# Input projections of a two-layer encoder trunk: the 512 columns of a matmul walked in alternating ways instead of in order

## The chip, the cores and the metric

The kernel runs on one core of one Trainium2 chip. The metric is the device time of one execution, in microseconds (us), smaller is better.

## What is computed

Two residual layers over a stream `x` of 256 tokens by 2048 columns, all in fp32. Each layer norms the stream, multiplies it by one combined input projection, runs a token mixer (layer 0: differential attention with 16 heads; layer 1: a spatial gating MLP) and, beside it, a 4-head attention into 256 memory tokens, and maps both back by one output projection. A SwiGLU feed-forward part follows.

```python
for i in range(DEPTH):                      # DEPTH = 2
    h = rms_norm(x, norm_mix_g[i])          # (256, 2048)
    mem_n = rms_norm(mem, norm_mem_g[i])
    if m == 0:
        p = h @ a_w_in[j]                   # 2048 x (6144 + 512)
        tok = diff_attention(p[..., :A_PROJ], ...)
        xq, w_out = p[..., A_PROJ:], a_w_out[j]
    elif m == 1:
        p = h @ b_w_in[j]                   # 2048 x (4096 + 512)
        tok = spatial_gating_mlp(p[..., :B_PROJ], ...)
        xq, w_out = p[..., B_PROJ:], b_w_out[j]
    cross = memory_attention(xq, mem_n, ...)
    x = x + jnp.concatenate([tok, cross], axis=-1) @ w_out
    x = x + swiglu(rms_norm(x, norm_ffn_g[i]), ffn_w_gate[i], ffn_w_up[i], ffn_w_down[i])
```

The two lines `p = h @ ...` are the input projections.

## The kernel before

**Number format.** A product of two fp32 matrices is made of three matmuls in a rounded fp32 type (`F32R`, fp32r in the profile): each factor is split into a high part and a low part, and high by high, high by low and low by high are summed in PSUM.

**Blocks.** The output columns of a projection are cut into blocks of 512, the width of one PSUM bank of fp32. Layer 0 has 13 blocks (`A_BLOCKS`: one for the memory queries, then four groups of keys, queries, values), layer 1 has 9 (`B_BLOCKS`). A block runs over 8 chunks (`IN_CHUNKS`) of the contraction; a chunk is two tiles of 128 rows of weights, 512 KB. For each chunk, `product` issues 2 contraction tiles x 2 token tiles x 3 matmuls = 12 matmuls, so a block has 96 and the 22 blocks have 2112. In each of them the stationary operand is a 128x128 tile of the transposed stream (`hT_hi`, `hT_lo`), the moving operand is 128 rows by 512 columns of split weights (`w_hi` or `w_lo`), read in order of address, and the result is added into the 512 columns of a bank, in order of address. `run_block` also issues, between chunks, the transposes and the attention steps that belong to earlier blocks.

**Supply.** The order of all instructions is written out by hand, engine by engine. SyncE loads a chunk of raw weights into a ring of four places, ScalarE rounds it to `w_hi` (L1061), VectorE subtracts to get `w_lo` (L1504), and TensorE waits for `chunk_split` before the first matmul of a chunk. Its last matmul counts up `chunk_used`, which lets ScalarE and VectorE write that place again. The banks of a block are read by ScalarE and VectorE while TensorE works on the next block in two others; these reads don't look at the order in which the columns were written.

The same function `product` also serves the key and value projections of the memory, the output projection of layer 0 and most units of the feed-forward part. In all of these the columns are taken in order.

Of the kernel before, what the change touches and what calls it, by code (L numbers as in the profile page):

```python
# [51 lines left out]
IN_CHUNKS = KT // CHUNK_KT  # L52
# [39 lines left out]
END_SUM_T = (END_SUM[1] + 1, END_SUM[1] + 3)  # L92
AHEAD = 3
HOOK = 4
CROSS_HOOK = 7


# [136 lines left out]
def trunk(nc, x, mem, rel_bias, norm_mix_g, norm_mem_g, norm_ffn_g, mem_w_kv, mem_q_norm_g,  # L234
# [4 lines left out]
    with ctx:  # L239
# [13 lines left out]
        w_hi = sb("w_hi", [P, RING, CHUNK_KT, BLOCK], F32R)  # L253
        w_lo = sb("w_lo", [P, RING, CHUNK_KT, BLOCK], F32R)
# [131 lines left out]
        bank = [ctx.enter_context(nc.psum_tensor(f"bank{i}", [P, BLOCK], F32)) for i in range(8)]  # L386
# [76 lines left out]
        def ring_place(tally):  # L463

            n = tally.n["chunk"]
            ring_turn = n // RING
            if tally.turn is not None:
                ring_turn = tally.turn * (tally.per_turn["chunk"] // RING) + ring_turn
            return ring_turn, n % RING
# [45 lines left out]
        def layer_steps(layer, b, cross_step, diff_step):  # L515


            if b in ((2, 3), (3, 4))[layer]:
                return (lambda c: cross_step(IN_CHUNKS * (b - 2 - layer) + c)) if cross_step else None, CROSS_HOOK
            if layer == 0 and b >= 4:  # L520
                group, third = divmod(b - 4, 3)
                return (lambda c: diff_step(group, IN_CHUNKS * third + c)), DIFF_HOOKS[third]
            return None, HOOK

        def outputs_due(layer, b):

            if (layer, b) in ((0, 4), (1, 5)):
                return [("cross_out", layer)]
            if layer == 0 and b in (7, 10):
                return [("outputs", (b - 7) // 3)]  # L530
            return []
# [73 lines left out]
        def _(pe):  # L605
# [3 lines left out]

            asked = dict(cross_scores=0, diff_scores=0, transposed=0)  # L610

            def product(side_T, outs, c, order, first, last_one, ready=(), token_first=False):

                hi, lo = side_T
                _, slot = ring_place(tally)
                pe.wait_ge(chunk_split, tally.at("chunk", 1))
                if c in ready:
                    pe.wait_ge(T_free, tally.at("t"))  # L620
                steps = [(a, t) for a in range(CHUNK_KT) for t in range(TOK)]
                if token_first:
                    steps.sort(key=lambda at: at[1])
                for a, t in steps:
                    k = order[c] * CHUNK_KT + a
                    rows = slice(t * P, (t + 1) * P)
                    o = bank[outs[t]][:, :]
                    nc.tensor.matmul(o, hi[:, k, rows], w_hi[:, slot, a, :], start=(first and a == 0), stop=False)  # L628
                    nc.tensor.matmul(o, hi[:, k, rows], w_lo[:, slot, a, :], start=False, stop=False)  # L629
                    last = nc.tensor.matmul(o, lo[:, k, rows], w_hi[:, slot, a, :], start=False,  # L630
                                            stop=(last_one and a == CHUNK_KT - 1))
                    if token_first and (a, t) == (CHUNK_KT - 1, 0):
                        last.then_inc(first_token_done, 1)
                last.then_inc(chunk_used, 1)
                tally.add("chunk")
# [100 lines left out]
                                                v_b[:, t, h * P:(h + 1) * P], start=True, stop=True)  # L736
                last.then_inc(mixed, 1)

            def run_block(previous, side_T, chunks, ready=(), steps=None, hook=HOOK, order=None, end=False):

                base = 2 * parity[0]
                parity[0] ^= 1
                for c in range(chunks):
                    if steps is not None:
                        steps(c)
                    for kind, j in previous:
                        if kind == "gated":
                            if c == hook:
                                mix(j)
                            elif c == hook + 2:  # L750
                                transpose4(y_tile)
                        elif c == hook:
                            after(kind, j)
                    product(side_T, (base, base + 1), c, order or range(chunks), c == 0, c == chunks - 1, ready,
                            token_first=(end and c == chunks - 1))


            def three(o, hi, lo, weight_hi, weight_lo, first, last_one):
# [170 lines left out]
            stream_T = (hT_hi, hT_lo)  # L929
# [55 lines left out]
            previous = [("mem_values", 1)]  # L985

            for layer, blocks in enumerate((A_BLOCKS, B_BLOCKS)):
                for b, (kind, j, _) in enumerate(blocks):
                    steps, hook = layer_steps(layer, b, lambda at: cross_step(layer, at), diff_step)
                    previous += outputs_due(layer, b)  # L990

                    run_block(previous, stream_T, IN_CHUNKS, ((0,) if layer == 0 else (6,)) if b == 0 else (), steps, hook)
                    previous = [(kind, j)]

                if layer == 0:

                    previous += [("outputs", QT - 2)]
                    bases = (2 * parity[0], 2 * (parity[0] ^ 1))
                    for i, (b, c) in enumerate(TAIL_CHUNKS):
                        diff_step(QT - 1, i, tail_steps)  # L1000
                        if i == HOOK + 1:
                            for p in previous:
                                after(*p)
                        product(mixer_T, (bases[b], bases[b] + 1), c, OUT_ORDER, c == 0, False, (0, OUT_SPARE) if b == 0 else ())
                    diff_step(QT - 1, 2 * OUT_EARLY, tail_steps)


                    wait(pe, s_free, HEADS)
                    t_banks[0] = O_BANKS
                    bases += (T_BANKS,)  # L1010
                    for i, (b, c) in enumerate(END_CHUNKS):
                        if i == END_TRANSPOSE:
                            after("outputs", QT - 1)
                        if i in END_SUM_T:
                            after("stream", END_SUM_T.index(i))
                        product(mixer_T, (bases[b], bases[b] + 1), c, OUT_ORDER, c == 0, c == OUT_CHUNKS - 1,
                                (OUT_EARLY,) if b == 0 else ())
                    t_banks[0] = T_BANKS
                    run_block([("stream", 2)], mixer_T, OUT_CHUNKS, order=OUT_ORDER)
                    banks = (2 * parity[0], 2 * (parity[0] ^ 1))  # L1020
                    events = {HOOK: [("stream", 3)]}
                else:
                    banks = (2 * parity[0], 2 * (parity[0] ^ 1))
                    run_pair(PAIRS + 1, OUT[0], mixer_T, out_sets[0], banks, {HOOK: [("mix", QT - 1)], HOOK + 2: [("gated", QT - 1)]},
                             fresh=True, order=OUT_ORDER)
                    run_pair(PAIRS, OUT[1], mixer_T, out_sets[1], banks, {OUT_HOOKS[0]: [("stream", 0)], OUT_HOOKS[1]: [("stream", 1)]},
                             fresh=True, order=OUT_ORDER)
                    events = {OUT_HOOKS[0]: [("stream", 2)], OUT_HOOKS[1]: [("stream", 3)]}

                run_pair(0, plan_of(0), stream_T, buffers(0), banks, events, fresh=True)  # L1030
                hidden = {GATE_HOOK: [("hidden", 0)]}
                with pe.Fori(0, (LATE - 2) // TURN_PAIRS) as turn:
                    tally.enter(turn)
                    for pair in (1, 2):
                        run_pair(pair, plan_of(pair), stream_T, buffers(pair), banks, hidden)
                    tally.leave((LATE - 2) // TURN_PAIRS)
                for pair in range(LATE - 1, PAIRS):
                    run_pair(pair, plan_of(pair), stream_T, buffers(pair), banks, hidden)
                run_pair(PAIRS, DOWN[0], hidden_T, down_sums[0], banks, hidden, fresh=True)
                if layer == 0:  # L1040
                    events = {HOOK: [("stream", 0)], DOWN_NEXT: [("stream", 1)],
                              DOWN_DONE_T: [("collected", 0), ("stream", 2)]}
                else:
                    events = {DOWN_NEXT: [("final", 1)]}
                run_pair(PAIRS + 1, DOWN[1], hidden_T, down_sums[1], banks, events, fresh=True, end=(layer == 1))
                parity[0] ^= 1
                previous = [("stream", QT - 1)]
# [1130 lines left out]
```

## Time and profile before

| | |
|---|---|
| median of 2 runs | 2346.77 us (2346.41 to 2347.14) |
| span of the profiled execution | 2345.2 us, from its first to its last instruction |
| TensorE (PE) busy in it | 2338.7 us |
| VectorE (DVE) busy | 1828.8 us |
| ScalarE (ACT) busy | 1267.7 us |
| DMA | 449.52 MB, mean 192 GB/s |

The profile is of one execution of its own. It gives the span; no other time of that execution is given, so the span stands for it, 1.6 us under the median of the runs. A line such as "L628 PE MATMUL bank<-w_hi,hT_hi 128*128 128x512 f32 x1600" is a group of instructions: line of the kernel, engine, operation, what is written and read, the stationary tile, the moving tile, and how many there are. The duration of a matmul in such a line runs from its start to the end of its drain, and the next one starts before that. How long the engine needs per matmul is therefore read from the distance between two starts in the timeline.

### The profile page before, as it was taken

How to read it: one execution, taken by the hardware profiler on the slowest of the kernel's cores; microseconds unless marked ns; L12 is line 12 of the kernel's file. 1: busy time of each engine (PE TensorE's matmuls, PEld its weight loads, DVE VectorE, ACT ScalarE, POOL GpSimd, SP SyncE). 2: the span in 40 equal slices, each digit the busy share in tenths (PEclk: the TensorE clock that was granted, in tenths of full speed). 3: DMA queues.
4: the chain of work that ended last, by engine and by line, in shares of the span. 5: the costliest groups of instructions: out<-in, count | busy, mean ns of one | idle time of the engine just before them, and what ended most of it. 6: DMA issues, size and time to landing. Idle time of an engine off the chain costs nothing.

```text
span 2345.2 us, 29322 instructions
## 1 busy us (share of the span) xinstructions
PE 2338.7 (100%) x10530; PEld 1895.1 (81%) x10530; DVE 1828.8 (78%) x2257; ACT 1267.7 (54%) x1572; POOL 171.3 (7%) x120
## 2 busy tenths in 40 slices
PE   9999999999999999999999999999999999999999
PEld 7888888888888888888888888888888888888887
DVE  6555666656988888889998546689988888889987
ACT  7645555545655555555564454455655555555553
POOL 1000110000111121110000000000111111100000
PEclk9999999999999999999999999999999999999999
DMA  8665555456665666666656755556665666667664
GB/s 262 208 188 154 162 162 162 157 167 205 205 191 188 198 194 188 200 195 227 198 184 201 234 157 167 179 180 202 206 202 185 198 191 187 198 196 227 201 206 156
DMA packets 235043, 449.52 MB, mean 192 GB/s; under 512 B 14893, under 2 KB 19122, under 8 KB 234674
## 3 DMA queue, kind: packets, MB, share of 16 engines
q1 hardware_dynamic: 224274, 430.01, 58.4%
q10 hardware_dynamic: 10656, 18.00, 2.2%
q8 instruction: 71, 1.16, 0.2%
q14 instruction: 42, 0.34, 0.0%
HBM read 441.64 MB, written 6.32 MB: 191 GB/s over the span
## 4 chain that ended last, share of the span: by engine, by line
PE 98%; ACT 1%; DVE 1%; issue 0%; POOL 0%; ACTq 0%; POOLq 0%; DVEq 0%
PE bank L630 24%; PE bank L628 24%; PE bank L629 24%; PE bank L759 7%; PE bank L761 7%; PE bank L760 7%; PE bank L684 2%; PE bank L881 1%; PE bank L649 0%; PE bank L906 0%; PE bank L735 0%; PE bank L855 0%; PE bank L830 0%; ACT w_hi L1061 0%; PE bank L893 0%
## 5 line engine op out<-in xcount | busy, mean ns | idle before, releaser
L1504 DVE TENSOR_TENSOR w_lo<-raw,w_hi 128x1024 fp32r<-128x1024 f32 (+1 forms) x816 | 951.0, 1181 | 443.7 <-ACT w_hi L1061 441.6
L1061 ACT ACTIVATE w_hi<-raw 128x1024 fp32r<-128x1024 f32 (+1 forms) x815 | 812.9, 1007 | 754.2 <-PE bank L630 704.1
L628 PE MATMUL bank<-w_hi,hT_hi 128*128 128x512 f32 x1600 | 639.2, 400 | 0.0
L630 PE MATMUL bank<-w_hi,hT_lo 128*128 128x512 f32 x1600 | 635.0, 397 | 0.0
L629 PE MATMUL bank<-w_lo,hT_hi 128*128 128x512 f32 x1600 | 630.7, 394 | 0.0
L630 PEld LDWEIGHTS bank<-w_hi,hT_lo 128*128 128x128 f32 x1600 | 300.4, 188 | 71.8
L629 PEld LDWEIGHTS bank<-w_lo,hT_hi 128*128 128x128 f32 x1600 | 300.7, 188 | 71.4
L628 PEld LDWEIGHTS bank<-w_hi,hT_hi 128*128 128x128 f32 x1600 | 300.5, 188 | 69.5
L628 PE MATMUL bank<-w_hi,aT_hi 128*128 128x512 f32 x864 | 344.6, 399 | 0.0
L630 PE MATMUL bank<-w_hi,aT_lo 128*128 128x512 f32 x864 | 341.4, 395 | 0.0
L629 PE MATMUL bank<-w_lo,aT_hi 128*128 128x512 f32 x864 | 340.5, 394 | 0.0
L630 PEld LDWEIGHTS bank<-w_hi,aT_lo 128*128 128x128 f32 x864 | 162.2, 188 | 40.1
L629 PEld LDWEIGHTS bank<-w_lo,aT_hi 128*128 128x128 f32 x864 | 162.3, 188 | 38.2
L628 PEld LDWEIGHTS bank<-w_hi,aT_hi 128*128 128x128 f32 x864 | 162.2, 188 | 37.7
L1067 ACT ACTIVATE aT_hi<-sum_raw 128x2048 fp32r<-128x2048 f32 x52 | 99.5, 1914 | 76.7 <-DVE sum_raw L1524 75.2
L1531 DVE TENSOR_TENSOR aT_lo<-sum_raw,aT_hi 128x2048 fp32r<-128x2048 f32 x52 | 119.0, 2289 | 8.2 <-ACT aT_hi L1067 8.2
L2106 POOL TENSOR_TENSOR sum_raw<-raw 128x1024 f32<-128x1024 f32 x16 | 39.6, 2475 | 571.4 <-DMA raw<-in_ffn_w_up_dram 571.4
L2134 POOL TENSOR_TENSOR pow_out<-pow_in,halves 128x8 f32<-128x8 f32 (+1 forms) x16 | 40.8, 2552 | 397.0 <-DVE pow_in L1572 397.0
L759 PE MATMUL bank<-aT_hi,mix_hi 128*128 128x512 f32 x174 | 69.0, 397 | 0.0
L760 PE MATMUL bank<-aT_lo,mix_hi 128*128 128x512 f32 x174 | 68.8, 395 | 0.0
L761 PE MATMUL bank<-aT_hi,mix_lo 128*128 128x512 f32 x174 | 68.7, 395 | 0.0
L2134 POOL TENSOR_TENSOR rstd<-pow_in,halves 128x2 f32<-128x2 f32 x6 | 5.5, 914 | 757.5 <-DVE pow_in L1572 757.5
(237 smaller groups left out, 2595.0 us busy)
## 6 DMA issues: line engine op xcount, KB each, us to landing
raw<-in_ffn_w_gate_dram SPq DMA_DIRECT2D x176, 512.0 KB, 3.8
raw<-in_ffn_w_up_dram SPq DMA_DIRECT2D x176, 512.0 KB, 4.5
raw<-in_ffn_w_down_dram SPq DMA_DIRECT2D x176, 512.0 KB, 4.6
raw<-in_a_w_in_dram SPq DMA_DIRECT2D x104, 512.0 KB, 3.8
raw<-in_b_w_in_dram SPq DMA_DIRECT2D x72, 512.0 KB, 3.8
raw<-in_a_w_out_dram SPq DMA_DIRECT2D x40, 512.0 KB, 3.7
raw<-in_b_w_out_dram SPq DMA_DIRECT2D x40, 512.0 KB, 4.2
raw<-in_mem_w_kv_dram SPq DMA_DIRECT2D x32, 512.0 KB, 5.1
```

The lines of the kernel that those rows point to most:

```text
L628: nc.tensor.matmul(o, hi[:, k, rows], w_hi[:, slot, a, :], start=(first and a == 0), stop=False)
L629: nc.tensor.matmul(o, hi[:, k, rows], w_lo[:, slot, a, :], start=False, stop=False)
L630: last = nc.tensor.matmul(o, lo[:, k, rows], w_hi[:, slot, a, :], start=False, stop=(last_one and a == CHUNK_KT - 1))
L684: last = nc.tensor.transpose(ktile(t_banks[0], a)[:, t * P:(t + 1) * P], tile(t, a), ident[:, :])
L759: nc.tensor.matmul(o, hi, weight_hi, start=first, stop=False)
L760: nc.tensor.matmul(o, hi, weight_lo, start=False, stop=False)
L761: return nc.tensor.matmul(o, lo, weight_hi, start=False, stop=last_one)
L1061: nc.scalar.activation(w_hi[:, slot, 0:tiles], raw[:, slot, 0:tiles], ACT.Copy).then_inc(hi_ready, 1)
L1067: nc.scalar.activation(weights[0], weights[2][:, :, :], ACT.Copy).then_inc(sums_hi, 1)
L1504: nc.vector.tensor_tensor(w_lo[:, slot, 0:tiles], raw[:, slot, 0:tiles], w_hi[:, slot, 0:tiles].bitcast(F32), ALU.subtract).then_inc(chunk ...
L1531: nc.vector.tensor_tensor(lo, total[:, :, :], hi.bitcast(F32), ALU.subtract).then_inc(sums_split, 1)
L2134: nc.gpsimd.tensor_tensor(dest, pow_in[:, q % 2, 0:count], halves[:, 0:count], ALU.pow).then_inc(pow_given, 1)
```

## The change

A table `WALKS` gives each block of the input projections a walk: None, or a pair (ways, run). `walked` views the 512 columns as `ways` equal parts, and takes `run` neighbouring columns of the first part, then `run` of the second, and so on, then the next `run` of the first. The moving operand and the bank are both walked so, so each column still meets its own sum. Nothing else is changed: the stationary operand, the number of matmuls and the order of all instructions stay.

Of the 22 blocks three have None. In three more, (2, 256), (4, 128) and (8, 64), ways x run is 512, so each part is taken whole and the order is that of the addresses. The other 16 blocks jump: layer 0 from its third block on with (2, 128), (2, 64), (2, 32), (2, 16), (2, 8), (2, 4), (2, 2), (4, 16), (4, 2), (8, 2), (16, 2), and layer 1 in its third to seventh block with (4, 32), (4, 8), (8, 16), (16, 16), (32, 2).

```diff
+WALKS = ((None, (2, 256), (2, 128), (2, 64), (2, 32), (2, 16), (2, 8), (2, 4), (2, 2), (4, 16), (4, 2), (8, 2), (16, 2)),
+         (None, (4, 128), (4, 32), (4, 8), (8, 16), (16, 16), (32, 2), (8, 64), None))
...
-            def product(side_T, outs, c, order, first, last_one, ready=(), token_first=False):
+            def walked(columns_of, walk):
+
+                if walk is None:
+                    return columns_of
+                ways, run = walk
+                return columns_of.rearrange("p (h r c) -> p r h c", h=ways, c=run)
+
+            def product(side_T, outs, c, order, first, last_one, ready=(), token_first=False, walk=None):
...
-                    o = bank[outs[t]][:, :]
-                    nc.tensor.matmul(o, hi[:, k, rows], w_hi[:, slot, a, :], start=(first and a == 0), stop=False)
-                    nc.tensor.matmul(o, hi[:, k, rows], w_lo[:, slot, a, :], start=False, stop=False)
-                    last = nc.tensor.matmul(o, lo[:, k, rows], w_hi[:, slot, a, :], start=False,
+                    o = walked(bank[outs[t]][:, :], walk)
+                    weights_hi, weights_lo = (walked(w[:, slot, a, :], walk) for w in (w_hi, w_lo))
+                    nc.tensor.matmul(o, hi[:, k, rows], weights_hi, start=(first and a == 0), stop=False)
+                    nc.tensor.matmul(o, hi[:, k, rows], weights_lo, start=False, stop=False)
+                    last = nc.tensor.matmul(o, lo[:, k, rows], weights_hi, start=False,
                                             stop=(last_one and a == CHUNK_KT - 1))
...
-            def run_block(previous, side_T, chunks, ready=(), steps=None, hook=HOOK, order=None, end=False):
+            def run_block(previous, side_T, chunks, ready=(), steps=None, hook=HOOK, order=None, end=False, walk=None):
...
-                    run_block(previous, stream_T, IN_CHUNKS, ((0,) if layer == 0 else (6,)) if b == 0 else (), steps, hook)
+                    run_block(previous, stream_T, IN_CHUNKS, ((0,) if layer == 0 else (6,)) if b == 0 else (), steps, hook,
+                              walk=WALKS[layer][b])
```

What TensorE is given, in the block of layer 0 with walk (2, 2): three matmuls of one contraction tile and one token tile. In the changed kernel the lines have moved (L628 to L630 are L640 to L642), and the last part of a row is the shape of the moving operand. Before:

```order
L630 MATMUL bank<-w_hi,hT_lo 128x512
L628 MATMUL bank<-w_hi,hT_hi 128x512
L629 MATMUL bank<-w_lo,hT_hi 128x512
```

Now:

```order
L642 MATMUL bank<-w_hi,hT_lo 128x128x2x2
L640 MATMUL bank<-w_hi,hT_hi 128x128x2x2
L641 MATMUL bank<-w_lo,hT_hi 128x128x2x2
```

No row moved, came or went: the 512 columns became 128 rounds over 2 ways of 2 columns.

## Rows read from the trace of the kernel before

**Rows 1.** The page: span, busy time by engine, TensorE's rows by slice
```profile
span 2345.2 us, 29322 instructions
PE 2338.7 (100%) x10530; PEld 1895.1 (81%) x10530; DVE 1828.8 (78%) x2257; ACT 1267.7 (54%) x1572; POOL 171.3 (7%) x120
...
PE   9999999999999999999999999999999999999999
...
PEclk9999999999999999999999999999999999999999
```

**Rows 2.** The page: the chain that ended last, by engine
```profile
PE 98%; ACT 1%; DVE 1%; issue 0%; POOL 0%; ACTq 0%; POOLq 0%; DVEq 0%
```

**Rows 3.** Windows over the jumping blocks: engine busy us (count), clock, DMA
```profile
157.00:433.00 276.00, 276.00 (x1352) 225.12 (x1351) 172.22 (x328) 145.90 (x260) 29.20 (x10) 1.00 0.54 160
1297.00:1527.00 230.00, 230.00 (x1080) 188.42 (x1079) 132.88 (x173) 108.90 (x136) 3.94 (x3) 1.00 0.61 186
```

**Rows 4.** Timeline of TensorE in a block of layer 0: start, duration, what
```profile
401.96 0.83 PE L906 MATMUL bank<-v_a,at_T 128*128 128x128 f32 x6
402.72 0.92 PE L881 MATMUL bank<-kT,qT 64*128 64x256 f32 x8
...
404.14 0.40 PE L630 MATMUL bank<-w_hi,hT_lo 128*128 128x512 f32 x1
404.38 0.39 PE L628 MATMUL bank<-w_hi,hT_hi 128*128 128x512 f32 x1
404.61 0.39 PE L629 MATMUL bank<-w_lo,hT_hi 128*128 128x512 f32 x1
...
408.34 0.40 PE L630 MATMUL bank<-w_hi,hT_lo 128*128 128x512 f32 x1
```

**Rows 5.** Timeline of TensorE early on, matmuls of 256 columns
```profile
8.94 1.12 PE L649 MATMUL bank<-w_hi,aT_lo 128*128 128x256 f32 x8
9.90 1.11 PE L649 MATMUL bank<-w_lo,aT_hi 128*128 128x256 f32 x8
```

**Rows 6.** Groups by line and form: weight loads and the split of weights
```profile
L628 PEld LDWEIGHTS bank<-w_hi,hT_hi 128*128 128x128 f32 x1600 | 300.5, 188 | 69.5
...
L1504 DVE TENSOR_TENSOR w_lo<-raw,w_hi 128x1024 fp32r<-128x1024 f32 (+1 forms) x816 | 951.0, 1181 | 443.7 <-ACT w_hi L1061 441.6
L1061 ACT ACTIVATE w_hi<-raw 128x1024 fp32r<-128x1024 f32 (+1 forms) x815 | 812.9, 1007 | 754.2 <-PE bank L630 704.1
```

**Rows 7.** Waits: who waited for whom, us in total, times, longest
```profile
ACT w_hi L1061 <- PE bank L630: 704.1, 467, 4.6
...
PE bank L937 <- POOL ident L2123: 1.6, 1, 1.6
...
PEld bank L684 <- DVE y L1591: 1.8, 2, 1.5
PE bank L684 <- DVE y L1591: 1.0, 1, 1.0
```

More of the change, by code:

```diff
@@ L754, in run_block @@
                     product(side_T, (base, base + 1), c, order or range(chunks), c == 0, c == chunks - 1, ready,
-                            token_first=(end and c == chunks - 1))
+                            token_first=(end and c == chunks - 1), walk=walk)
             def three(o, hi, lo, weight_hi, weight_lo, first, last_one):
```

## The prediction, made before the changed kernel ran

> **What bounds the kernel now.** I read four views in this order. The page's first part shows TensorE busy for 2338.7 of 2345.2 us, at full granted clock in every slice [rows 1]; full clock is the 2.4 GHz level. The chain of waits that ended last lies on TensorE for 98% [rows 2]. The windows over the blocks that the change touches show TensorE busy for all of 276 and all of 230 us, with VectorE at 172 of 276 and 133 of 230 [rows 3]. The waits show where the slack is: ScalarE waited 704.1 us in all for matmuls to release the places it writes, while TensorE's own waits are 1.6 and 1.0 us [rows 7]. So in these stretches a nanosecond more or less per matmul on TensorE goes into the end one for one, and nothing else in the change touches another engine.
>
> The busy share cannot say how long a matmul holds the engine, because neighbours overlap. The timeline can: 18 matmuls of 512 columns start between 404.14 and 408.34 us, so the distance is 4.20 / 18 = 0.2333 us [rows 4]. Eight matmuls of 256 columns start between 8.94 and 9.90 us, 0.120 us each [rows 5]. The second 256 columns thus cost 0.1133 us, **0.443 ns a column**, and about 7 ns are left per matmul for everything that doesn't depend on the columns. A matmul here is paced by its stream of columns, not by its weight load, which takes 188 ns [rows 6] in matmuls of 512 columns 233 ns apart, and goes on at 120 ns spacing with 256 columns. This matters: the change touches only that stream.
>
> **The change part by part.** It removes and adds no instruction and moves none. Six of the 22 blocks keep their order of columns (None three times, and three walks whose parts are taken whole); they cost nothing, since the same addresses follow in the same order. Sixteen blocks jump: 16 x 96 = 1536 matmuls, 1536 x 0.2333 = 358 us of the 2345. Eleven of them lie in layer 0 (the 276 us of the first window and a few behind it), five in layer 1.
>
> What a jump costs is the one unknown. No matmul in the trace of before reads or writes its columns in jumps: every moving tile and every bank is taken in order. So I bound it.
>
> From below: the whole distance is 0.2333 us and 512 columns at 2.4 GHz would be 0.2133 us. If a walk took away all that lies between, it would gain 0.020 us a matmul, 1536 x 0.020 = 31 us. There is no row that shows such a gain by an order of columns; the end is kept because the 20 ns have no owner in the trace.
>
> From above: the slowest stream of columns in the trace is that of plain fp32 matmuls, six records of 128 columns in 402.72 - 401.96 = 0.76 us [rows 4], 0.127 us each, 0.99 ns a column. If every column of a jumping block cost that, it would be 512 x (0.99 - 0.443) = 0.280 us more per matmul, 1536 x 0.280 = 430 us.
>
> Between these ends far apart I take **zero**. The nearest row is the one of the same instruction with 512 columns, and what differs is only the address sequence. All walks keep runs of at least two fp32 columns, 8 bytes, that begin at an even column, on the reading and on the writing side alike. The stream is one column every 0.443 ns, slightly slower than the clock's 0.417 ns, so the engine is already fed with a small reserve of clock cycles. An address that jumps needs no more instruction words, and issuing is not the limit: the engine starts matmuls every 0.120 us where they are short [rows 5].
>
> The Trainium skill (Advanced Engine Details and Errata, section Memory Cachelines) says that an SBUF line of 16 bytes needs two hits to be read at full rate, and that in PSUM, with lines of 8 bytes, every two consecutive elements should be contiguous. By that rule all walks here are free, since the shortest run is two fp32 values. The same section and PSUM — Partial Sum Buffer (Specifications (TRN2)) also say that any non-contiguous access pattern slows matmuls significantly. By this second rule the sum would be hundreds of microseconds; it is the third rival below. No row of before can decide between the two.
>
> Beside TensorE: ScalarE's rounding takes 1.007 us and VectorE's subtraction 1.181 us per chunk [rows 6], against 12 x 0.2333 = 2.80 us of matmuls. They stay hidden if matmuls grow, and also if these shrink by 9%. The evacuations read banks that are complete; their order isn't touched. DMA is at 0.54 to 0.61 [rows 3] and is released by the splits; it has no term. The sum is 2345.2 + 0 = 2345.2 us of span, and with the 1.6 us by which the median of the runs stands above it, 2346.8. I say **2347 us**.
>
> **The rivals.**
>
> *A charge for every run (slower).* The place is the address generation or the memory port at each jump, and the price is paid once per run. Runs in a matmul are 512 / run; over the sixteen walks they sum to 4 + 8 + 16 + 32 + 64 + 128 + 256 + 32 + 3 x 256 in layer 0 and 16 + 64 + 32 + 32 + 256 in layer 1, together 1708, times 96 matmuls is 163,968 runs. At the time of one column, 0.443 ns, that is 72.6 us: 2419 us. It decides the verdict from 46.9 us on (2% of the time), 0.286 ns a run. For it: the stream already runs a little behind the clock, so something in the feed takes extra cycles now. Against it: the price per column is nearly that of the clock, and nothing in the trace shows a cost at a boundary.
>
> *Only runs of two pay (slower).* If memory delivers four fp32 columns at a time and a run of two wastes half, the five walks with run 2, 480 matmuls, take twice the stream: 480 x 512 x 0.443 ns = 109 us, 2456 us; at the 0.99 ns of the slowest row it would be 480 x 0.280 = 134 us, 2481 us. For it: 0.443 ns is close to a full rate, so a half-used access would have no reserve. Against it: nothing in the trace shows the size of an access.
>
> *Every jumping walk streams at half rate (much slower).* 1536 x 512 x 0.443 ns = 348 us, 2695 us, or 2777 us at the row above. That is the mechanism which the skill's second rule would mean here. Walks whose runs are 128 or 64 columns jump 4 or 8 times in a matmul, and for these it seems out of proportion.
>
> *The walk helps (faster).* At most 31 us, 2316 us, as worked out above; 1.3%, so still within 2%. Small gains of a few us are likelier than the whole of it.
>
> *The change doesn't do what it says.* If the order of columns were brought back to that of the addresses before it reaches the engine, the time would stay at 2347 us. The rows of the changed program speak against it: they carry the shapes of the walks.
>
> **How the numbers follow.** Chances: no cost 0.58; a charge per run 0.22, of which 0.14 above the 2% bound; runs of two only 0.09; half rate for all 0.04; a gain 0.06, of which 0.01 beyond 2% for what I can't price; not as said 0.01. Two per cent is about what a measurement of this kernel can tell from no change. Faster by over 2%: 0.01. Within 2%: 0.58 + 0.01 + 0.08 + 0.05 = 0.72. Slower by over 2%: 0.14 + 0.09 + 0.04 = 0.27. The predicted time is that of the likeliest case. The range starts at 2338, a gain of a few us, and reaches over the charge per run at one column (2419) to 2425; it holds 0.58 + 0.01 + 0.22 and some of the gain, a little over 0.8. It leaves out the two heavier cases and the larger gains. The likeliest case's own range is 2343 to 2351.
>
> **What would show it.** In the profile of the changed kernel the distance of starts in each block is the test, since each block has a walk of its own. No cost: 0.233 us in all 22. A charge per run: 0.233 in the block with (2, 128), growing with the number of runs to 0.233 + 256 x 0.443 ns = 0.347 us in the five with runs of two, whatever the ways. Runs of two only: a step to about 0.46 us in those five and none elsewhere, with (2, 4) free. Half rate for all: about 0.46 us in sixteen blocks. If the distance depends on the ways at one run (2, 4, 8, 16 and 32 ways have runs of two), the cost sits in the distance of the jump and none of my cases has it. If TensorE's distances stay and the time grows, there would be a new wait on TensorE before the first matmul of a chunk. The forecast is wrong if any walk costs over 0.1 us a matmul.

## The result and the profile after

The changed kernel takes **2444.35 us** (median of 2 runs, 2443.95 to 2444.75), against 2346.77 before: a ratio of 1.0416, 95% interval 1.0386 to 1.0447. It is 97.6 us slower; the forecast was 2347 us, with a range up to 2425.

The page of the kernel after, lines that answer to [rows 1] and [rows 2]:

```profile
span 2442.9 us, 29322 instructions
PE 2435.7 (100%) x10530; PEld 1903.3 (78%) x10530; DVE 1829.3 (75%) x2257; ACT 1268.3 (52%) x1572; POOL 169.5 (7%) x120
...
PE   9999999999999999999999999999999999999999
PEld 7888765468888888888888887688888888888887
...
PEclk9999999999999999999999999999999999999999
...
PE 98%; ACT 1%; DVE 1%; issue 0%; DMA 0%; SPq 0%; POOL 0%; ACTq 0%; DVEq 0%
```

The span grew by 97.7 us and TensorE's busy time by 97.0, at the same count of instructions and the same full clock. VectorE and ScalarE have the busy time they had. The row of weight loads shows where: its share falls to 4 tenths near the end of layer 0's blocks and to 6 in layer 1's, for the loads are as many and as long as before and the matmuls beside them are longer. Two windows around the blocks of [rows 3] (stretch, its length, busy us with counts of TensorE, weight loads, VectorE, ScalarE and GpSimd, then clock, DMA share, GB/s):

```profile
157.00:519.00 362.00, 362.00 (x1389) 238.84 (x1388) 176.46 (x329) 149.52 (x262) 27.30 (x10) 1.00 0.44 127
1364.00:1623.00 259.00, 259.00 (x1120) 197.86 (x1120) 138.40 (x179) 113.40 (x143) 3.94 (x3) 1.00 0.57 170
```

TensorE is busy in all of both. They are 86 and 29 us longer than those of [rows 3], but they also hold 37 and 40 matmuls more, so the growth of the blocks is not read from them; it is 78 us in layer 0 and 20 us in layer 1, by the table of blocks below. In the groups by line the change is nearly invisible, for a group mixes the blocks with all other products of the line; this is TensorE's first one before, and then the same one after, with ScalarE's rounding:

```profile
L628 PE MATMUL bank<-w_hi,hT_hi 128*128 128x512 f32 x1600 | 639.2, 400 | 0.0
...
L640 PE MATMUL bank<-w_hi,hT_hi 128*128 128x512 f32 x1600 | 675.4, 422 | 0.0
...
L1074 ACT ACTIVATE w_hi<-raw 128x1024 fp32r<-128x1024 f32 (+1 forms) x815 | 813.4, 1008 | 847.8 <-PE bank L642 795.1
```

The timeline of a single block shows it. Start and duration of TensorE's matmuls in layer 0's block with walk (4, 2), then in the one with (8, 2); compare the starts in [rows 4], 0.233 us apart:

```profile
380.94 0.62 PE L640 MATMUL bank<-w_hi,hT_hi 128*128 128x512 f32 x1
381.38 0.62 PE L641 MATMUL bank<-w_lo,hT_hi 128*128 128x512 f32 x1
...
385.38 0.62 PE L641 MATMUL bank<-w_lo,hT_hi 128*128 128x512 f32 x1
...
426.78 0.67 PE L640 MATMUL bank<-w_hi,hT_hi 128*128 128x512 f32 x1
427.26 0.67 PE L641 MATMUL bank<-w_lo,hT_hi 128*128 128x512 f32 x1
...
430.19 0.67 PE L641 MATMUL bank<-w_lo,hT_hi 128*128 128x512 f32 x1
```

Ten distances take 385.38 - 380.94 = 4.44 us, 0.444 each; seven take 3.41 us, 0.487 each. No semaphore wait lies between: the engine streams the same 512 columns for about twice the time.

Taken for every block, from the start of its first matmul to that of the next block's, minus the same block before, over the 96 matmuls of a block. "Distance" is how far the starts of successive runs lie apart in the weights, 2048 bytes over the ways:

| walk | distance, bytes | ns more per matmul | us in the block |
|---|---|---|---|
| (2, 128), (2, 64) | 1024 | 0.0, 0.0 | 0.0 |
| (2, 32), (2, 16), (2, 8) | 1024 | 3.5, 6.7, 10.1 | 0.34, 0.64, 0.97 |
| (2, 4) | 1024 | 22.6 | 2.17 |
| (2, 2) | 1024 | 102.2 | 9.81 |
| (4, 32), (4, 16), (4, 8) | 512 | 0.2, -1.5, -0.3 | 0.02, -0.14, -0.03 |
| (4, 2) | 512 | 211.0 | 20.26 |
| (8, 16) | 256 | 0.9 | 0.09 |
| (8, 2) | 256 | 254.0 | 24.38 |
| (16, 16) | 128 | 5.1 | 0.49 |
| (16, 2) | 128 | 203.4 | 19.53 |
| (32, 2) | 64 | 200.8 | 19.28 |

The five blocks with runs of two columns make 93.3 us, the other eleven 4.5. With two ways the price grows with the number of runs, from nothing for 4 and 8 runs in a matmul to 22.6 ns for 128; with four ways 16, 32 and 64 runs cost nothing. The blocks that keep the order of addresses differ by 1.2 ns at most.

### The profile page after: what moved, and what is told of

Read it like the earlier page. It is cut to its first block, busy times and chain, and to the rows that moved or that the text cites. A ratio compares the mean times of both kernels' runs of the same rounds, so it can differ in the third digit from the quotient of the medians.

```text
span 2442.9 us, 29322 instructions
## 1 busy us (share of the span) xinstructions
PE 2435.7 (100%) x10530; PEld 1903.3 (78%) x10530; DVE 1829.3 (75%) x2257; ACT 1268.3 (52%) x1572; POOL 169.5 (7%) x120
## 4 chain that ended last, share of the span: by engine, by line
PE 98%; ACT 1%; DVE 1%; issue 0%; DMA 0%; SPq 0%; POOL 0%; ACTq 0%; DVEq 0%
PE bank L642 25%; PE bank L640 25%; PE bank L641 24%; PE bank L771 6%; PE bank L773 6%; PE bank L772 6%; PE bank L696 2%; PE bank L893 1%; PE bank L661 0%; PE bank L918 0%; PE bank L747 0%; PE bank L867 0%; ACT w_hi L1074 0%; PE bank L842 0%; PE bank L905 0%
## 5 line engine op out<-in xcount | busy, mean ns | idle before, releaser
L1074 ACT ACTIVATE w_hi<-raw 128x1024 fp32r<-128x1024 f32 (+1 forms) x815 | 813.4, 1008 | 847.8 <-PE bank L642 795.1
L640 PE MATMUL bank<-w_hi,hT_hi 128*128 128x512 f32 x1600 | 675.4, 422 | 0.0
L642 PE MATMUL bank<-w_hi,hT_lo 128*128 128x512 f32 x1600 | 670.3, 419 | 0.0
L641 PE MATMUL bank<-w_lo,hT_hi 128*128 128x512 f32 x1600 | 667.8, 417 | 0.0
L642 PEld LDWEIGHTS bank<-w_hi,hT_lo 128*128 128x128 f32 x1600 | 303.4, 190 | 101.6 <-issue 31.7
L640 PEld LDWEIGHTS bank<-w_hi,hT_hi 128*128 128x128 f32 x1600 | 303.3, 190 | 96.9 <-issue 27.9
L640 PE MATMUL bank<-w_hi,aT_hi 128*128 128x512 f32 x864 | 343.5, 398 | 0.0
L642 PE MATMUL bank<-w_hi,aT_lo 128*128 128x512 f32 x864 | 341.9, 396 | 0.0
L642 PEld LDWEIGHTS bank<-w_hi,aT_lo 128*128 128x128 f32 x864 | 162.2, 188 | 39.1
L640 PEld LDWEIGHTS bank<-w_hi,aT_hi 128*128 128x128 f32 x864 | 162.2, 188 | 38.5
```

The costliest lines, as they stand in the source:

```text
L640: nc.tensor.matmul(o, hi[:, k, rows], weights_hi, start=(first and a == 0), stop=False)
L641: nc.tensor.matmul(o, hi[:, k, rows], weights_lo, start=False, stop=False)
L642: last = nc.tensor.matmul(o, lo[:, k, rows], weights_hi, start=False, stop=(last_one and a == CHUNK_KT - 1))
L1074: nc.scalar.activation(w_hi[:, slot, 0:tiles], raw[:, slot, 0:tiles], ACT.Copy).then_inc(hi_ready, 1)
```

## The experiments

The theories after the result: **M**, the price is on the reading side, where the weights come from SBUF; **B**, it is on the side of the PSUM bank. Later **M16**: the weights arrive in accesses of 16 aligned bytes, four fp32 columns, and an access takes the time of four columns however many of them are used. M16 is a model of the times; no view shows an access itself.

### The moving operand alone

```diff
-                    o = walked(bank[outs[t]][:, :], walk)
+                    o = bank[outs[t]][:, :]
```

> The moving operand is walked as in the change, the bank is written in order, so the columns of the projections come out permuted (that part of the computation is changed). Theory M (the price is on the reading side: a run of two fp32 columns uses half of what one access to the weights delivers): all of the change's 97.6 us stays, about 2444 us, and the blocks with (2, 2), (4, 2), (8, 2) show 0.335, 0.445 and 0.487 us between starts, as in the changed kernel. Theory B (the price is on the bank's side, where every column is added to what is there): 2347 us and 0.233 us in all blocks. If both sides charge and the slower one sets the pace, both one-sided kernels are slower, each by at most 98 us; if they add, their gains sum to 98 us.

Measured: 2444.47 us, ratio 1.0415 (1.0399 to 1.0431). TensorE in the block with (4, 2):

```profile
380.90 0.62 PE L642 MATMUL bank<-w_hi,hT_lo 128*128 128x512 f32 x1
...
386.23 0.62 PE L642 MATMUL bank<-w_hi,hT_lo 128*128 128x512 f32 x1
```

Twelve distances in 5.33 us, 0.444 us. Every block is within 0.2 ns a matmul of the changed kernel's. The whole price is on the reading side, as M has it.

### The bank alone

```diff
-                    weights_hi, weights_lo = (walked(w[:, slot, a, :], walk) for w in (w_hi, w_lo))
+                    weights_hi, weights_lo = (w[:, slot, a, :] for w in (w_hi, w_lo))
```

> The bank is walked as in the change, the moving operand is read in order, so the columns come out permuted the other way (that part of the computation is changed). Theory M: 2347 us, 0.233 us in all blocks. Theory B: about 2444 us, with 0.335, 0.445 and 0.487 us for (2, 2), (4, 2), (8, 2).

Measured: 2346.79 us, ratio 0.9999 (0.9990 to 1.0009). The same block:

```profile
368.69 0.39 PE L641 MATMUL bank<-w_lo,hT_hi 128*128 128x512 f32 x1
...
371.96 0.39 PE L640 MATMUL bank<-w_hi,hT_hi 128*128 128x512 f32 x1
```

Fourteen distances in 3.27 us, 0.234 us: nothing is paid for jumps in the bank, down to runs of two columns at any of the ways. B falls, and with it the Trainium skill's rule (PSUM — Partial Sum Buffer, Specifications (TRN2)) that any non-contiguous pattern slows matmuls significantly, as far as the bank's side and runs of at least two fp32 columns go. The measurement decides.

### Without the runs of two

```diff
-WALKS = ((None, (2, 256), (2, 128), (2, 64), (2, 32), (2, 16), (2, 8), (2, 4), (2, 2), (4, 16), (4, 2), (8, 2), (16, 2)),
-         (None, (4, 128), (4, 32), (4, 8), (8, 16), (16, 16), (32, 2), (8, 64), None))
+WALKS = ((None, (2, 256), (2, 128), (2, 64), (2, 32), (2, 16), (2, 8), (2, 4), None, (4, 16), None, None, None),
+         (None, (4, 128), (4, 32), (4, 8), (8, 16), (16, 16), None, (8, 64), None))
```

> The change with its five walks of run two put back to None; the eleven jumping walks with runs of 4 to 128 stay. If, as the distances of starts in the changed kernel say, the five blocks carry 93 of the 97.6 us: 2351 us (ratio 1.002). If the price were a charge per run, the eleven would keep 428 of 1708 runs, a quarter of the price: 2371 us.

Measured: 2351.37 us, ratio 1.0019 (1.0010 to 1.0028). The five blocks carry 93.0 of the 97.6 us; a charge per run falls.

### More walks

```diff
+WALKS = ((None, (2, 2), (4, 4), (8, 4), (16, 4), (32, 4), (64, 4), (8, 8), (16, 8), (32, 8), (64, 2), (128, 2), (4, 64)),
+         ((4, 2), (2, 2), (8, 32), (2, 64), (16, 2), (4, 8), (4, 4), (32, 4), None))
```

> Both sides walked, with another table: new pairs of ways and run, and six walks of the change in other blocks. Both theories: a walk costs the same wherever it stands, so (2, 2) adds 0.102 us a matmul in both of its blocks, (4, 2) 0.211, (16, 2) about 0.20. Theory M: a run of four fills an access, so the five walks (4, 4), (8, 4), (16, 4), (32, 4), (64, 4) and all with run 8 or more are within 0.01 us of 0.233, and (64, 2) and (128, 2), where two neighbouring runs lie 32 and 16 bytes apart, cost 0.2 us more like (16, 2). Theory B: what counts is the distance between successive runs, 2048 bytes over the ways; the price is largest near 8 ways and falls towards 128 ways for run 4 as for run 2, so (8, 4) and (16, 4) are clearly above 0.25 us.

Measured in one execution (its time, 2461.24 us, belongs to this mix of walks and says nothing by itself), ns more per matmul by distance in bytes. The rows are the lengths of the runs, and two figures are two blocks with the same walk:

| run | 1024 | 512 | 256 | 128 | 64 | 32 | 16 |
|---|---|---|---|---|---|---|---|
| 2 | 101.5, 95.3 | 211.8 | | 201.1 | | 226.2 | 219.9 |
| 4 | | 34.4, 34.7 | 44.5 | 15.1 | **-10.2, -2.1** | -0.2 | in order |
| 8 | | 0.3 | 13.7 | -2.4 | 0.2 | in order | |
| 32, 64 | 0.1 (64) | 0.4 (64) | 2.6 (32) | in order | | | |

The price belongs to the walk, not to the block: (4, 2) 211.0 and 211.8, (16, 2) 203.4 and 201.1, (4, 4) twice the same. Runs of two cost about one more matmul's stream at every distance but 1024 bytes. My sentence that all runs of four are free missed: at 128 to 1024 bytes they pay 15 to 44 ns (22.6 at 1024, by the table before), at 64 bytes they gain. (8, 8) with 13.7 ns is outside my 10 ns too. For runs of four the price is largest at 8 ways, as the sentence on B had it, but the bank alone has been shown to cost nothing, and for runs of two it doesn't fall towards 128 ways. The gaining block (32, 4) of layer 0, TensorE:

```profile
255.82 0.38 PE L642 MATMUL bank<-w_hi,hT_lo 128*128 128x512 f32 x1
...
259.34 0.38 PE L640 MATMUL bank<-w_hi,hT_hi 128*128 128x512 f32 x1
...
270.66 1.03 PE L696 MATMUL bank<-ident,y 128*128 128x128 f32 x8
...
272.91 0.39 PE L640 MATMUL bank<-w_hi,hT_hi 128*128 128x512 f32 x1
...
276.39 0.39 PE L640 MATMUL bank<-w_hi,hT_hi 128*128 128x512 f32 x1
```

Sixteen distances in 3.52 us, 0.220 us: faster than columns in order. But the same walk in the same block doesn't keep that rate. After the transposes (L696), 15 distances take 3.48 us, 0.232 each.

### Neighbouring runs of two, and where (32, 4) gains

```diff
+                if walk[0] == "back":
+                    lines = columns_of.rearrange("p (h r c) -> p r h c", h=walk[1], c=walk[2])
+                    return lines[:, :, ::-1, :]
+                if walk[0] == "swap":
+                    lines = columns_of.rearrange("p (r h c) -> p r h c", h=2, c=2)
+                    return lines[:, :, ::-1, :]
...
+WALKS = (((32, 4), (32, 4), None, (32, 4), ('swap',), None, (32, 4), ('back', 128, 4), ('back', 256, 2), ('back', 32, 4), (32, 4), (2, 2), (2, 4)),
+         ((32, 4), (32, 4), (2, 2), (2, 2), (32, 4), ('swap',), (32, 4), (32, 4), (32, 4)))
```

> Both sides walked, another table. (32, 4) stands in twelve blocks, for it gained 10 ns a matmul in the sixth block of layer 0 (0.223 us between starts) and only 2 ns in the eighth of layer 1 (0.232 us). If its gain depends on the layer (its data or its other traffic): 0.223 us in all six blocks of layer 0 that have it, 0.232 in all six of layer 1. If it depends on the pair of banks, which alternates from block to block: both values in both layers. New: the two halves of each 16 bytes swapped (columns 2, 3, 0, 1, 6, 7, 4, 5), and runs of two from the last to the first; both read each 16 bytes whole, by two neighbouring runs of two. Theory M16 (an access delivers 16 bytes; a run of two is dear because it wastes half of one): both within 0.01 us of 0.233. Rival (every run of two is dear in itself): 0.43 us or more in both. The order of addresses turned round in runs of four, and (32, 4) with its ways turned round: by M16 no more than 0.02 us from 0.233 and 0.223.

Measured in one execution (2373.54 us, again of a mix of walks): the swapped halves cost 0.2 and 0.0 ns a matmul, runs of two backwards 0.0. TensorE in the block with swapped halves:

```profile
212.62 0.39 PE L648 MATMUL bank<-w_hi,hT_lo 128*128 128x512 f32 x1
...
215.88 0.40 PE L647 MATMUL bank<-w_lo,hT_hi 128*128 128x512 f32 x1
```

Fourteen distances in 3.26 us. The same number of runs of two as in (4, 2), and nothing to pay: what counts is whether two neighbouring runs come out of the same 16 bytes. The rival falls, M16 stands. Turning the order round is free too (0.2 ns in runs of four; (32, 4) with its ways turned round gains 4.5). Three more blocks with (2, 2) paid 94 to 101 ns.

The gain of (32, 4) followed neither of the two explanations: -1.8, -2.0, -3.7, -4.4 and -5.0 ns in layer 0, -5.2, -6.7, -3.9, -2.2, -2.1 and -2.2 in layer 1, with the first two blocks, which use different pairs of banks, alike. I had also counted twelve such blocks; the table has eleven. What the traces do show is that the rate holds through a stretch and changes between stretches. In the kernel with (32, 4) in all input projections (below), 22 stretches have more than 30 matmuls in a row without another kind between. In each of them the mean over any twelve successive distances, after the first six, stays within 1 ns: at 0.232 us in nineteen, at 0.225 in two, at 0.220 in one. A block's gain is mostly the mix of these rates.

### Starting between two blocks of 16 bytes

```diff
+WALKS = ((None, (0, 480, None, None), None, (2, 480, None, None), (0, 480, 30, 4), (2, 480, 30, 4), (0, 480, 60, 4), (2, 480, 60, 4), (0, 480, 30, 8), (2, 480, 30, 8), (0, 480, 15, 16), (2, 480, 15, 16), (2, 480, 60, 2)),
+         ((0, 480, 60, 2), (0, 384, None, None), (0, 256, None, None), (0, 128, None, None), (0, 448, None, None), (0, 320, None, None), (0, 480, 15, 4), (2, 480, 15, 4), None))
...
-                ways, run = walk
-                return columns_of.rearrange("p (h r c) -> p r h c", h=ways, c=run)
+                first_col, width, ways, run = walk
+                part = columns_of[:, first_col:first_col + width]
+                if ways is None:
+                    return part
+                return part.rearrange("p (h r c) -> p r h c", h=ways, c=run)
```

> Matmuls of the input projections cut to a part of the columns (the others are left out of the sums), contiguous or walked, starting at column 0 or at column 2, so that each run of four straddles two blocks of 16 bytes. Theory M16 (the weights are read in aligned accesses of 16 bytes, each worth four columns of time, 1.8 ns): 480 columns in order cost the same from column 0 and from column 2 (about 0.219 us). In runs of four from column 0: within 0.02 us of that; from column 2 two accesses a run, twice the stream: 0.42 us. Runs of eight from column 2: three accesses for two, 0.32 us. Runs of 16 from column 2: five for four, 0.27 us. Runs of two 32 bytes apart: 0.42 us from either column. Rival (length of the run alone decides): the start changes nothing, and runs of four and more stay at 0.22 us. The widths 448, 384, 320, 256 in order show what a matmul costs beside its columns: with 0.443 ns a column and 7 ns beside them 0.205, 0.177, 0.148 and 0.120 us.

Measured in one execution (2411.15 us, with these columns left out), us between starts. "Accesses" counts the 16-byte blocks that the runs touch:

| 480 columns | from column 0 | accesses | from column 2 | accesses |
|---|---|---|---|---|
| in order | 0.220 | 120 | 0.215 | 121 |
| runs of 4, 64 bytes apart | 0.213 | 120 | **0.423** | 240 |
| runs of 4, 32 bytes apart | 0.219 | 120 | **0.426** | 240 |
| runs of 4, 128 bytes apart | 0.227 | 120 | **0.412** | 240 |
| runs of 8, 64 bytes apart | 0.218 | 120 | **0.308** | 180 |
| runs of 16, 128 bytes apart | 0.220 | 120 | **0.270** | 150 |
| runs of 2, 32 bytes apart | 0.433 | 240 | 0.433 | 240 |

TensorE with runs of four 64 bytes apart, from column 0 and then from column 2, and with runs of eight from column 2:

```profile
208.13 0.38 PE L644 MATMUL bank<-w_lo,hT_hi 128*128 128x480 f32 x1
...
211.33 0.38 PE L644 MATMUL bank<-w_lo,hT_hi 128*128 128x480 f32 x1
...
231.91 0.60 PE L643 MATMUL bank<-w_hi,hT_hi 128*128 128x480 f32 x1
...
236.96 0.60 PE L643 MATMUL bank<-w_hi,hT_hi 128*128 128x480 f32 x1
...
371.16 0.49 PE L645 MATMUL bank<-w_hi,hT_lo 128*128 128x480 f32 x1
...
373.96 0.47 PE L645 MATMUL bank<-w_hi,hT_lo 128*128 128x480 f32 x1
```

3.20 us over 15 distances, 5.05 over 12, 2.80 over 9. The number of columns, ways and runs is the same in the first two; only the start moved by 8 bytes, and the matmul takes twice the time. The bank is shifted here with the weights; but in the kernel with the bank alone walked, runs of two began at every even column, also in the middle of a block of 16 bytes, at no cost. That speaks for the weights here too; the bank alone was not shifted. Differences of 0.005 us in the table are no property of a walk: columns in order from column 2 stand at 0.213 us in most stretches and at 0.220 in one. The ratios of the straddling walks to 0.213 to 0.220 us, 2, 1.4 and 1.25, are those of the accesses (2, 1.5, 1.25). Less the 7 ns of [rows 5], an access takes 0.416 / 240 = 1.73 ns, 0.301 / 180 = 1.67, 0.263 / 150 = 1.75; in order it is 0.226 / 128 = 1.77 ns for four columns. The widths in order gave 0.205 us for 448 columns, 0.177 for 384, 0.147 for 320, 0.120 for 256, as forecast to 0.001 us. The table of walks also has 128 columns in order, for which the same formula gives 0.064 us:

```profile
1419.03 0.27 PE L644 MATMUL bank<-w_lo,hT_hi 128*128 128x128 f32 x1
...
1421.48 0.27 PE L645 MATMUL bank<-w_hi,hT_lo 128*128 128x128 f32 x1
```

22 distances in 2.45 us are 0.111 us each. So the formula ends between 256 and 128 columns, and something else sets the pace there; what it is, no run shows.

### Walk (32, 4) in the input projections, and everywhere

```diff
+WALKS = (((32, 4),) * 13, ((32, 4),) * 9)
```

and for the second also:

```diff
-            def product(side_T, outs, c, order, first, last_one, ready=(), token_first=False, walk=None):
+            def product(side_T, outs, c, order, first, last_one, ready=(), token_first=False, walk=(32, 4)):
...
-            def run_block(previous, side_T, chunks, ready=(), steps=None, hook=HOOK, order=None, end=False, walk=None):
+            def run_block(previous, side_T, chunks, ready=(), steps=None, hook=HOOK, order=None, end=False, walk=(32, 4)):
...
             def three(o, hi, lo, weight_hi, weight_lo, first, last_one):
+                o, weight_hi, weight_lo = (walked(x, (32, 4)) for x in (o, weight_hi, weight_lo))
```

> All 22 blocks of the input projections, and nothing else, take walk (32, 4): 2112 matmuls. At 10.2 ns each: 2347 - 21.5 = 2325 us. At 10.2 ns in layer 0 and 2.1 in layer 1: 2347 - 12.7 - 1.8 = 2332 us. If the two readings were not of the walk: 2347 us.

> All fp32r matmuls of 512 columns but those of the first memory block take walk (32, 4): runs of 16 bytes, 64 bytes apart, on both sides. 9408 of them in the trace of before. If each gains 10.2 ns as in layer 0's block: 96 us, 2251 us, less what the splits on VectorE and ScalarE then hold up in the feed-forward part, where VectorE is busy for nine tenths. If each gains 2.1 ns as in layer 1's block: 20 us, 2327 us.

Measured: 2338.76 us, ratio 0.9965 (0.9951 to 0.9978), and 2309.93 us, ratio 0.9845 (0.9831 to 0.9858). That is 8.2 us over 2112 matmuls and 37.0 over 9408, 3.9 ns each in both. Of the times forecast, neither of the two for all matmuls (2251 and 2327) nor any of the three for the input projections (2325, 2332, 2347) came; the 10.2 ns of the one block came from a long stretch at 0.220 us and is not the walk's mean gain. In the first of the two kernels the blocks lie between -1.8 and -6.7 ns.

### Walk (16, 8) everywhere

The same edit with (16, 8).

> As the kernel that had walk (32, 4) everywhere (2310 us), with (16, 8) in its place: runs of 32 bytes, 128 bytes apart. It gained 2.4 ns a matmul in one block; on 9408 matmuls that is 23 us, 2324 us. If its gain was a chance of that block: 2347 us.

Measured: **2298.96 us**, ratio 0.9795 (0.9779 to 0.9811), the fastest of all: 48.0 us, 5.1 ns a matmul, twice what the one block had shown; the forecast of 2324 us missed by 25 us. TensorE in the first block of layer 0:

```profile
106.31 0.39 PE L641 MATMUL bank<-w_hi,hT_lo 128*128 128x512 f32 x1
...
109.48 0.39 PE L640 MATMUL bank<-w_lo,hT_hi 128*128 128x512 f32 x1
```

Fourteen distances in 3.17 us, 0.226 us. Its 22 blocks gain between 2.6 and 8.0 ns.

## Why the prediction was wrong

**What bounds the kernel** was right. TensorE was and stayed the bound, and each added nanosecond of a matmul is in the result: the block lengths sum to 97.7 us, the time grew by 97.6. The distance between starts as the measure of a matmul, 0.443 ns a column and 7 ns beside them, held over five widths from 256 to 480 columns, and not at 128.

**The failed step** is "Between these ends far apart I take **zero**". Its reason, that only the address sequence differs, was an assumption that the address sequence doesn't matter. The reserve that I read out of 0.443 against 0.417 ns is none: the contiguous stream already takes one 16-byte access per four columns, and an access takes 1.67 to 1.77 ns (1.88 in (8, 2): 0.480 us / 256), so an access that delivers two columns halves the rate. A run of 8 bytes at an even start is not enough; whole aligned blocks of 16 bytes are, but for the 15 to 44 ns that runs of four pay at some distances. I leaned here on the agreement with the Trainium skill (Advanced Engine Details and Errata, Memory Cachelines), by which two hits on a line give full rate. For the fp32r columns of these matmuls this is not what the runs show: two hits per access give half the rate, four the full one.

**The rival that came true** is "Only runs of two pay". It had the right mechanism, even the 16 bytes, and got 0.09. Its price was 109 us for five blocks at 0.227 us a matmul; they cost 93.3, because four of them pay 0.201 to 0.254 and (2, 2) only 0.102. What I held against it, that nothing in the trace shows the size of an access, was equally no argument for zero. I split the chance by how familiar the mechanisms seemed, and the trace could not tell the two apart. The other half of its statement, (2, 4) free, is off by 2.2 us.

**The upper bound** was sixteen blocks at the 0.99 ns a column of six records of 128 columns. That row was misread: matmuls of 128 columns in order stand 0.111 us apart in fp32r too, so it says little about the price of a column. The forecast didn't lean on it.

**A charge for every run** is wrong as a rule: (2, 64) has 8 runs and (2, 128) 4 at no cost, and the swapped halves have 256 runs at none. **Half rate for all** is wrong. **The walk helps** was right in kind. In the change only (4, 16) gained clearly, 1.5 ns; (16, 8) and (32, 4), which it doesn't contain, gain more. The bound of 20 ns a matmul was never passed: 5.1 were had as a mean, 13 in the stretch at 0.220 us.

**The rest of the working.** ScalarE's and VectorE's splits stayed hidden, with ScalarE's wait for matmuls grown from 704.1 to 795.1 us. DMA and evacuations had no term, and none is missing, for the blocks' lengths account for the whole change.

**What stays open.** Why two ways 1024 bytes apart with runs of two pay half the price (each 16 bytes are touched again after one other access); why full accesses at distances of 128 to 1024 bytes pay up to 44 ns, and that in no order of distance; and why (16, 8) and (32, 4) beat the order of addresses. That the gain changes from block to block is neither the layer nor the pair of banks. With (32, 4) the rate changes where other matmuls come between and otherwise stays, so it looks like something that is set when a stretch starts; what it is, and whether it can be chosen, was not tried. With (16, 8) some stretches hold 0.227 us and others wander between 0.218 and 0.241 us.

## What to carry to other kernels

For an fp32r matmul lay the moving operand so that every run of columns starts on a 16-byte boundary and takes whole blocks of 16 bytes, and measure the distance between runs that you need, for some cost up to 44 ns of 233. The walk of the PSUM bank is free down to runs of two, so permute pairs of columns there. Where a stream of such matmuls is the bound, try the moving operand in runs of 32 bytes 128 bytes apart (and the bank alike): that took 2% off this kernel without another instruction. And give each block of a loop its own variant when a price is unknown: one profile then holds a map, where a mean over a line shows 400 ns becoming 422.

## What the runs showed of the hardware

- An fp32r matmul's time goes by the aligned blocks of 16 bytes that the runs of its moving operand touch, 1.67 to 1.77 ns each in most walks: 480 columns in runs of four take 0.213 us from column 0 and 0.423 from column 2. The model leaves three things over: (2, 2) takes 0.336 us for 256 blocks, (8, 2) 0.487 us, and (8, 4) 0.278 us for 128.
- Two neighbouring runs of two within the same 16 bytes count as one such block, also backwards: 0.0 to 0.2 ns more a matmul than in order.
- Jumps within a PSUM bank cost nothing, with accumulation, at 2 to 32 ways and runs of 2 to 128: ratio 0.9999 (0.9990 to 1.0009).
- Columns in order are not the fastest stream: 0.2333 us for 512, against 0.226 in the stretch shown with (16, 8), and 0.220, 0.225 or 0.232 with (32, 4), where the rate stays through a stretch of matmuls and changes between stretches.
- 128 columns in order take 0.111 us, where 0.443 ns a column and 7 ns would be 0.064.
